# Gated delta recurrence inside a five-layer network: the next head's keys and values turned in the last block

## What is computed

```
proj = h @ w_in                                   # q, k, v, z of all heads, beta, decay
qkv = silu(causal_conv(qkv, w_conv))
k = k * rsqrt(sum(k*k) + EPS);  q likewise
L = strict_lower((k*beta) @ k.T * decay)          # in chunks of C tokens
T = solve(I + L);  u = T @ (v*beta);  w = T @ (k*beta*exp(g))
qk = causal(q @ k.T * decay)
...
v_new = u_c - w_c @ state                         # one chunk after another
o     = qd @ state + qk_c @ v_new
state = state*exp(g_last) + kd.T @ v_new
...
o = o * rsqrt(mean(o*o) + EPS) * w_onorm
return (o * silu(z)) @ w_out
```

## Time and profile before

| | |
|---|---|
| median of 3 runs | 1987.19 us (1985.98 to 1990.04) |
| profiled execution, its own time | 1989.37 us |
| span in the profile | 1987.6 us |
| TensorE busy | 1966.1 us (99%) |
| VectorE busy | 1443.8 us (73%) |
| ScalarE busy | 558.4 us (28%) |
| GpSimd busy | 347.7 us (17%) |
| mean granted TensorE clock | 0.997 |
| one head of the recurrence | some 40.05 us, from 546 to 860 us of the span |

### The profile page before, as it was taken

One profiled execution on the slowest core, in us unless ns is written; L12 is line 12 of the kernel. 1 busy time (PEld: TensorE's weight loads), 2 busy tenths in 40 slices (PEclk: granted clock), 3 DMA queues, 4 the chain that ended last, 5 costly groups with the idle time before them and its releaser, 6 DMA issues.

```text
span 1987.6 us, 31469 instructions
## 1 busy us (share of the span) xinstructions
PE 1966.1 (99%) x12774; PEld 1587.3 (80%) x12774; DVE 1443.8 (73%) x2209; ACT 558.4 (28%) x1069; POOL 347.7 (17%) x317
## 2 busy tenths in 40 slices
PE   9999999999999999999999999999999999999999
PEld 8888888887777877777888877777888888888887
DVE  6666766677877777678997887675656779759963
ACT  2000122222433343234874244673300010000000
POOL 2111111111111111011111211111112222222221
PEclk9999999999999999999999999999999999999999
DMA  5333323222222121122222333111223333323332
GB/s 183 96 96 97 96 85 96 85 85 66 85 61 61 60 65 60 55 85 83 66 75 75 120 99 96 58 59 59 70 95 97 111 95 96 106 85 100 93 99 91
DMA packets 52192, 171.26 MB, mean 86 GB/s; under 512 B 6328, under 2 KB 6584, under 8 KB 51920
## 3 DMA queue, kind: packets, MB, share of 16 engines
q1 hardware_dynamic: 48112, 161.33, 26.2%
q10 hardware_dynamic: 3936, 7.92, 1.4%
HBM read 167.07 MB, written 2.15 MB: 85 GB/s over the span
## 4 chain that ended last, share of the span: by engine, by line
PE 51%; DVE 5%; ACT 1%; issue 1%; DVEq 0%; ACTq 0%
PE ps_lin L1931 15%; PE ps_lin L1933 14%; PE ps_lin L1932 14%; PE ps_att L1980 3%; PE ps_aux L1980 2%; DVE arena L431 1%; DVE arena L437 1%; PE ps_att L1989 1%; ACT arena L1345 1%; DVE w_lo L431 1%; DVE arena L434 0%; PE ps_lin L1951 0%; DVE arena L980 0%; PE ps_lin L1952 0%; PE ps_lin L1953 0%
## 5 line engine op out<-in xcount | busy, mean ns | idle before, releaser
L1931 PE MATMUL ps_lin<-xw_hi,w_hi 128*128 128x512 f32 x1704 | 690.0, 405 | 2.0 <-DVE w_lo L431 1.9
L1933 PE MATMUL ps_lin<-xw_hi,w_lo 128*128 128x512 f32 x1704 | 666.4, 391 | 0.0
L1932 PE MATMUL ps_lin<-xw_lo,w_hi 128*128 128x512 f32 x1704 | 665.4, 391 | 0.0
L413 POOL TENSOR_SCALAR w_hi<-raw 128x1024 fp32r<-128x1024 f32 (+2 forms) x309 | 343.8, 1113 | 1621.8 <-PE ps_lin L1933 1498.1
L431 DVE TENSOR_TENSOR w_lo<-raw,w_hi 128x1024 fp32r<-128x1024 f32 (+2 forms) x340 | 379.3, 1118 | 45.4 <-POOL w_hi L413 17.5
L1345 ACT ACTIVATE arena<-arena 128x512 f32<-128x512 f32 (+9 forms) x336 | 196.0, 591 | 699.9 <-DVE arena L431 325.7
L1931 PEld LDWEIGHTS ps_lin<-xw_hi,w_hi 128*128 128x128 f32 x1704 | 321.2, 188 | 69.4 <-issue 3.5
L1933 PEld LDWEIGHTS ps_lin<-xw_hi,w_lo 128*128 128x128 f32 x1704 | 320.6, 188 | 68.9
L1932 PEld LDWEIGHTS ps_lin<-xw_lo,w_hi 128*128 128x128 f32 x1704 | 321.5, 189 | 59.0
L431 DVE TENSOR_TENSOR arena<-ps_lin,rstd 128x512 f32<-128x512 f32 (+3 forms) x220 | 147.6, 671 | 190.7 <-PE ps_lin L1933 182.4
L1931 PE MATMUL ps_lin<-y_hi,w_hi 128*128 128x512 f32 (+1 forms) x544 | 205.3, 377 | 0.0
(11 more groups left out here) (189 smaller groups left out, 1653.2 us busy)
## 6 DMA issues: line engine op xcount, KB each, us to landing
raw<-in_w_up SPq DMA_DIRECT2D x44, 512.0 KB, 3.6
raw<-in_conv_w_in SPq DMA_DIRECT2D x32, 512.0 KB, 3.7
raw<-in_fox_w_in SPq DMA_DIRECT2D x32, 512.0 KB, 3.6
raw<-in_gdn_w_in SPq DMA_DIRECT2D x32, 512.0 KB, 3.6
raw<-in_w_gate SPq DMA_DIRECT2D x24, 512.0 KB, 3.6
raw<-in_swa_w_in SPq DMA_DIRECT2D x20, 512.0 KB, 3.6
raw<-in_w_ml SPq DMA_DIRECT2D x16, 512.0 KB, 3.6
raw<-in_w_down SPq DMA_DIRECT2D x16, 512.0 KB, 3.5
```

The costliest lines, as they stand in the source:

```text
L413: pool.tensor_scalar(w_whole(n, kc * c)[0], w_raw(n, kc * c), 1.0, 0.0, mult, add).then_inc(s("w_rounded"), 1)
L1931: pe.matmul(o, wh, hi, start=first and k == 0, stop=False)
L1932: pe.matmul(o, wh, lo, start=False, stop=False)
L1933: ins = pe.matmul(o, wl, hi, start=False, stop=last and k == kc - 1)
```

## The change

Four edits of order, all of them in the recurrence:

- the step between `gdn_w` and block 0 is gone from heads 0 to 6 (`fill(1)` only where `h == GDN_H - 1`);
- in block 3 of heads 0 to 6 the step is replaced by the next head's 8 transpositions (`gdn_keys(h + 1)`, `gdn_values(h + 1)`), which leave the front of heads 1 to 7. The two displaced steps are done at the end of the round, after `gdn_out`;
- `gdn_squares(h - 1)` stands after the eight steps of the front and directly ahead of the products of keys;
- since the next keys now lie in Y while block 3 is worked on, vn of block 3 goes to V (bank 3) in heads 0 to 6, on TensorE and in VectorE's copy.

```diff
-                    dve.tensor_copy(blk(F["vn"], c), blk(ps_att[:, 2 if c == 2 else 1, :], c)).then_inc(s("gdn_vn_out"), 1)
+                    dve.tensor_copy(blk(F["vn"], c), blk(ps_att[:, (1, 1, 2, 3 if h < GDN_H - 1 else 1)[c], :], c)).then_inc(s("gdn_vn_out"), 1)
...
+            def gdn_keys(h):
+
+                pe.wait_ge(s("gdn_silu"), 3 * h + 2)
+                for c in range(NT):
+                    last = tr(blk(ps_att[:, 1, :], c), blk(F["k"][:, h % 2, :], c))
+                last.then_inc(s("gdn_tok"), 1)
+
+            def gdn_values(h):
+
+                pe.wait_ge(s("gdn_silu"), 3 * h + 3)
+                for c in range(NT):
+                    last = tr(blk(ps_att[:, 2, :], c), blk(F["v"][:, h % 2, :], c))
+                last.then_inc(s("gdn_tok"), 1)
...
                 fill(1)
-                pe.wait_ge(s("gdn_vn_out"), NT * h)
-                pe.wait_ge(s("gdn_silu"), 3 * h + 2)
-                for c in range(NT):
-                    last = tr(blk(Y, c), blk(k_, c))
-                last.then_inc(s("gdn_tok"), 1)
+                if h == 0:
+                    gdn_keys(0)
                 fill(GDN_FILL["tok"] - 1)
                 if h == 0:
                     gdn_columns()
-                pe.wait_ge(s("gdn_nw"), h)
-                pe.wait_ge(s("gdn_silu"), 3 * h + 3)
-                for c in range(NT):
-                    last = tr(blk(Z, c), blk(v_, c))
-                last.then_inc(s("gdn_tok"), 1)
+                    gdn_values(0)
+                fill(GDN_FILL["squares"])
+                fill(GDN_FILL["A"])
                 if h:
                     gdn_squares(h - 1)
-                fill(GDN_FILL["squares"])
-                fill(GDN_FILL["A"])
...
-                W = (Y, Y, Z, Y)
+                W = (Y, Y, Z, V if h < GDN_H - 1 else Y)
...
-                fill(1)
+                if h == GDN_H - 1:
+                    fill(1)
...
-                    if c == NT - 1:
+                    if c == NT - 1 and h == GDN_H - 1:
                         fill(1)
+                    elif c == NT - 1:
+                        gdn_keys(h + 1)
+                        gdn_values(h + 1)
                     pe.wait_ge(s("gdn_vn_out"), NT * h + c + 1)
```

More of the change, by code:

```diff
@@ L2108, in four @@
                 return last
+            def gdn_keys(h):
[8 more added lines that the diff above has]
+                last.then_inc(s("gdn_tok"), 1)
             def gdn_head(h, fill):
-                q_, k_, v_ = (F[n][:, h % 2, :] for n in "qkv")
+                q_, k_ = (F[n][:, h % 2, :] for n in "qk")
                 X, Y, Z, V = (ps_att[:, i, :] for i in range(4))
```

## The result

The changed kernel takes **1993.03 us** (median of 6 runs, 1991.45 to 1995.18) where the kernel before takes 1987.07 us beside it (6 runs, 1985.06 to 1990.04): a ratio of 1.0026, with a 95% interval of 1.0017 to 1.0036. Slower by 6 us; 1992.9 us was forecast.

The account below looks back on a forecast made before the run. TensorE was taken as busy throughout, with VectorE's ring pacing blocks 1 and 2. The terms 0.27 + 3.10 + 0.60 + 1.72 = 5.7 us, added to a median of 1987.2, gave 1992.9 us; range 1989.3 to 1997.

Parts of the forecast that it names:

- The mechanism of the step: Ahead of block 0, heads 1 to 6: removed step is owed later, block 3 reached only 0.07 us earlier; 0.62 us lost.
- the joined groups in the front: Front of a head: changing between steps and 128-wide products costs nothing by itself, so fewer changes gain nothing.
- the first head: Block 0 of the first head: nothing is split, so the update starts 0.42 us earlier; loss 0.27 us.
- The ring: Blocks 1 and 2: VectorE's chain of update, state, half a w_lo and vn copy takes 1.98 us and sets the pace.
- The X wait: Level 1, heads 1 to 6: VectorE comes late to the first X; 0.1 us a head, ends 0 and 0.4.
- the z tile's delay: End of a round: the z tile's last step, and VectorE's evacuation with it, comes 1.72 us later.
- The last head: From the z tile's evacuation on, VectorE has no idle time, so the whole shift of 1.72 us arrives.
- the squares' 0.77 us: Last head: the squares' wait for VectorE's sum goes, but its 0.77 us are waited for again later.
- The sum: Whole kernel: first head, heads 1 to 6, level 1 and last head together cost 5.7 us.
- A second slow stretch: First rival, last head: the clock falls again or waits add up; 9.2 us slower, 1996.4 us; chance 0.2.
- the second rival: Last head and level 1: late z tile absorbed, no wait at X; 3.2 us slower, 1990.4 us; chance 0.17.
- the third: Rival, fronts of heads: fewer changes between steps and 128-wide products make the kernel faster, 1983.0 us; chance 0.04.

Follow-up runs that it names:

- e1: Kernel before, with only the step between the w products and block 0 left out in heads 0 to 6 and done at the round's end: 1993.45 us.
- e2: Changed kernel with the step between the w products and block 0 put back in all heads: 1991.94 us, ratio 1.0015.
- e4: Kernel before with VectorE's two halves of w_lo kept out of blocks 0 and 1 and done after block 3's copy: 1993.3 us, ratio 1.0025.
- e8: Kernel before with TensorE's output product done a block later, next block's u and the step directly behind the update: 1989.4 us, ratio 1.0005.
- e5: Changed kernel with VectorE's split of the earlier output moved from block 0 to after block 3's copy: 1993.8 us, ratio 1.0029.
- e3: Kernel before with only the squares' product moved to directly ahead of the products of keys: 1988.94 us, ratio 1.0002.
- e9: Kernel before with vn's first product of block 3 done in block 1 and the next head's key transpositions in block 2: 1986.61 us, ratio 0.9989.
- e10: Changed kernel with late split and late tap, old places of steps and transpositions in head 6's round and the last head's front: 1987.96 us, ratio 0.9998.
- e6: Changed kernel with VectorE's first convolution tap of the next q tile moved from ahead of the first X to behind it: 1992.41 us, ratio 1.0020.
- e7: Changed kernel with the output's split moved to block 3 and one convolution tap moved behind the first X: 1990.39 us, ratio 1.0008.

## Why the prediction was right

**The mechanism of the step (0.62 us a head forecast, 0.37 measured, 0.46 in e1).** TensorE reaches the update earlier, waits for VectorE's copy, and owes the step: shown by e1. Two numbers in it were off. Block 1 was to have its copy 0.10 us earlier than before; against Y0 it came 0.22 earlier (650.72 - 1.97 = 648.75, before 648.97), because VectorE started it before the row of the instruction ahead had ended: half a `w_lo` and the copy after it start 0.60 us apart, though the row says 0.69. And the joined groups in the front gave 0.09 us (e2), which the prediction had put at nothing. In the first head the term was 0.27 and measured 0.17.

**The ring.** The copies of blocks 1 and 2 did stay 2.0 us apart. The reason given was wrong: the sum of 1.98 us with half a `w_lo` in it fits by luck. e4 refutes it, and so does block 2 of the kernel before, with 2.07 us and no half in it. e8 says nothing on it, since VectorE's ring would have given 2.01 us as well. The last head shows the chain of hand-overs that takes its place.

**The X wait (0.1 us forecast with ends at 0 and 0.4; 0.30 and 0.04 measured).** The range held it, the value chosen was too small. But the two misses belong together. The prediction had TX 0.70 us later a head (667.8 against 667.10); measured are 669.79 - 1.97 = 667.82. VectorE sets that start: its z tile came 1.57 us later (forecast 1.72) and 0.61 us of idle time took some of it (forecast 0.73), so that the first X came 0.96 us later and not 0.99. XT, which is TensorE's, came only 0.44 us later instead of 0.62, and the wait at TX is longer by about that much. The terms were divided at the wrong place: the loss of a head at TX is the z tile's delay less VectorE's idle time behind it. That the sum, 0.72 us against 0.71, is right to the hundredth is luck as well, for the delay was 0.15 us too large and the idle time 0.12. It is also not so that the blocks' loss is always swallowed there: in e5 the blocks are 0.2 us shorter, the z tile comes as much earlier with them, and the wait at TX stays.

**The last head (1.72 forecast, 1.59 measured).** The mechanism holds row for row: no slack on VectorE from the z tile's evacuation on, the squares' 0.77 us waited for again (e3: last 20.25 both times), the step behind them with 1.28 us (forecast more than 1.3). Idle time grew by 1.1 us as forecast, but a step ahead of the squares took 1.20 us of it, which was not foreseen. The 0.13 us less are the z tile's: it came 1.59 us later against Y0 (821.62 - 811.65, 814.69 - 806.31), and all of that arrived.

**The sum.** 5.7 us forecast, 5.7 us of fixed part; the profiled executions differ by 4.7 us in span, and the medians by 6.0 (interval 3.4 to 7.2). The sum has no term for the waits in the levels nor for the slow stretch, and these were +1.0 and -1.4 us in the profiled pair; that the medians come so near to it owes something to luck. The head-to-head distance was to be 40.7 to 40.8 us; 16.00 + 4.65 + 1.57 + 18.52 = 40.74 without "issue" waits, a median of 41.0 us with them. Against the end of the w products block 1 starts 0.29 us earlier where less than 0.25 was said.

**The rivals.** A second slow stretch didn't come; rather the one that was there is absent from this execution. e8 has one more, in its first head (granted clock 0.93 in 550 to 555 us and 0.73 in 555 to 560), so such a stretch does occur, but no run ties it to the change. The 3.2 us of the second rival lie just outside the interval, and the X wait, which it puts at nothing, is there in every head. For the third, e2's 0.09 us a head is all that joining groups gives: the sign never hung on it.

**Left open.** Why heads 0 to 6 lose 0.85 us in all between TX and Y0 in one execution and 1.9 us or 4.5 us (e2) in another, "issue" waits among them; these are found in every kernel and no edit here was aimed at them. They blur a comparison of two profiles by more than most terms above.

## What to carry to other kernels

Where two engines hand results back and forth in a loop, find the pace of that loop in a place where neither has anything else to do; work that fits inside it is free, until one engine's own work is as long as the round (e9), and taking such work out only moves it to where it is paid. When the engine that feeds a wait is busy without a pause from some event on, cost a change by how much later that event comes, less the idle time behind it, rather than by a sum of TensorE's own delays. Before work is moved into an idle stretch, look at that stretch in every round (e10). And compare fixed distances head by head: with runs that spread over 4 us, four starts a head told apart terms of 0.04 us.

## What the runs showed of the hardware

- A hand-over between TensorE and VectorE and back, with a 128-wide product and a 128 x 128 operation twice each, takes 2.01 us (last head above), of which matmul passes at 0.11 us are the smallest part: from the update's start to the start of VectorE's work on it 0.60 us.
- Some of VectorE's rows overlap. Behind a half `w_lo` with a row of 0.69 us, the copy, which does not wait for it, starts after 0.60 us (650.12, 650.72); behind `y_lo`, for whose semaphore the program waits, the next starts after 0.73 us (649.06, 649.79). So rows added up can overstate a chain. With TensorE's order the same, an idle VectorE takes up the copy some 0.07 us later than a busy one: from the product for vn to the copy 0.49 us in e4 (653.99, 654.48) and 0.42 us before (650.56, 650.98).
- In the levels with products of 32 rows TensorE stops for "issue": 0.15 to 0.6 us in single heads, 1.4 us in the first head of e1 and e8, 1.6 us in the seventh of e2, and 1.45 to 2.2 us in the last head of all twelve profiled executions (1.89 at 840.80 above).
- The granted clock of 834 to 844 us was 0.83 before and 1.00 after, 0.83 in e1, 0.67 in e3, and 1.00 in e4 and e10. The Trainium skill (TensorE: Matmul & The Clock Gate, What's actually happening) has only the two levels, 1.2 and 2.4 GHz; a mean of 0.83 is then a part of the stretch at the lower one. In nine of the twelve profiled executions there is such a part, and in each it begins about where the last head's long "issue" wait ends (before: wait until 833.73, clock 0.66 from 834 to 839). In the other three (after, e4, e10) it is missing behind waits just as long (1.89, 1.55 and 1.86 us). From TX to Y0 the last head takes 16.8 to 17.0 us in those three and 17.8 to 19.8 us in the nine. With one profiled execution of each kernel it isn't shown what decides; e2, e5, e6 and e7 keep nearly the changed kernel's order and have the slow part, so nothing points to the change.
